# Moving the modulation sums of a four-layer block from VectorE to GpSimd

## The reference

```python
cond = jax.nn.silu(c)
for i in range(DEPTH):
    mod = (cond @ w_mod[i] + b_mod[i])[:, None, :]
    shift, scale, gate = jnp.split(mod, 3, axis=-1)
    h = rms_norm(x, norm_pre_g[i]) * (1.0 + scale) + shift
    o = mixer(h, ...)
    x = x + gate * rms_norm(o, norm_post_g[i])
```

```python
top_s, top_i = lax.top_k(s, PEER_TOPK)            # s: (T, heads, 2, 128)
cand_s = top_s[:, :, 0, :, None] + top_s[:, :, 1, None, :]
cand_i = top_i[:, :, 0, :, None] * 128 + top_i[:, :, 1, None, :]
best_s, pos = lax.top_k(cand_s, PEER_TOPK)        # over 256 candidates
idx = take_along_axis(cand_i, pos)
a = gelu(einsum('cd,ced->ce', x, expert_down[idx]))
out = einsum('ce,ced->cd', softmax(best_s) * a, expert_up[idx])
```

## Time and profile before

| | |
|---|---|
| median of 3 runs | 1738.4 us (1738.04 to 1740.64) |
| the profiled execution | 1739.41 us, its span 1737.6 us |
| TensorE busy | 1393.7 us, 80% |
| VectorE busy | 1047.5 us, 60% |
| ScalarE busy | 433.1 us, 25% |
| GpSimd busy | 490.7 us, 28% |
| DMA | 591.53 MB, mean 340 GB/s |

### The profile page before, as it was taken

How to read it: one execution, slowest core, us unless ns; L and a number is a source line. 1 busy time by engine, 2 the same in 40 slices (tenths; PEclk the granted TensorE clock), 3 DMA queues, 4 the chain that set the end, 5 groups by cost and what they waited for, 6 DMA issues and landing times. The chain is left out here.

```text
span 1737.6 us, 13867 instructions
## 1 busy us (share of the span) xinstructions
PE 1393.7 (80%) x4158; PEld 717.6 (41%) x4158; DVE 1047.5 (60%) x2197; ACT 433.1 (25%) x974; POOL 490.7 (28%) x498
## 2 busy tenths in 40 slices
PE   6998988978999999999777777699787647666665
PEld 6454435444444455444354343455333312222222
DVE  3645554553233222313797998788866778877876
ACT  1221413423423421102133232132002221111111
POOL 2101210210000000000445546355344545444441
PEclk9998998989999999999897888798888878898898
DMA  9978884978556776887999989999999999999995
GB/s 386 377 256 303 312 340 171 347 282 295 213 207 219 277 265 242 290 293 265 402 361 357 413 339 403 412 400 413 410 414 414 348 412 422 421 422 421 422 421 248
DMA packets 108941, 591.53 MB, mean 340 GB/s; under 512 B 12450, under 2 KB 12706, under 8 KB 60612
## 3 DMA queue, kind: packets, MB, share of 16 engines
q0 software_dynamic: 67776, 312.56, 45.4%
q1 hardware_dynamic: 41092, 278.10, 42.2%
HBM read 589.55 MB, written 1.05 MB: 340 GB/s over the span
## 5 line engine op out<-in xcount | busy, mean ns | idle before, releaser
L948 PE MATMUL bank<-ring,hT 128*128 128x512 f32 x1888 | 866.6, 615 | 39.6 <-DVE room L1920 12.1
L948 PEld LDWEIGHTS bank<-ring,hT 128*128 128x128 f32 x1888 | 366.5, 198 | 482.2 <-issue 449.8
L877 POOL DMA_INDIRECT room<-in_peer_down,idx x92 | 102.5, 1114 | 525.1 <-DVE idx L1781 401.8
L1798 DVE CUSTOM_DVE_ANT_0 room<-room 128x1024 f32<-128x1024 f32 x180 | 218.6, 1221 | 50.6 <-DMA room<-in_pair,idx 38.4
L1203 PE MATMUL bank<-room 128*128 128x512 f32 x284 | 150.9, 676 | 96.5 <-ACT room L1493 94.2
L1813 DVE SCALAR_TENSOR_TENSOR x<-room,pcoef,x 128x1024 f32<-128x1024 f32 x121 | 155.7, 1287 | 28.0 <-DMA room<-in_peer_up,idx 27.5
L877 POOL DMA_INDIRECT room<-in_peer_up,idx x104 | 114.0, 1096 | 88.6 <-DVE pa L1798 42.3
L1203 PEld LDWEIGHTS bank<-room 128*128 128x128 f32 x284 | 57.5, 215 | 190.8 <-issue 97.2
L849 POOL DMA_DIRECT2D room<-in_w_mod x80 | 42.2, 528 | 326.3 <-DVE room L1567 206.5
L877 POOL DMA_INDIRECT room<-in_pair,idx x88 | 97.0, 1102 | 108.5 <-PE bank L1203 50.6
L927 PE MATMUL bank<-cst,room 128*128 128x128 f32 x424 | 64.7, 297 | 55.3 <-ACT room L1439 24.1
(11 more groups left out here) (304 smaller groups left out, 1527.4 us busy)
## 6 DMA issues: line engine op xcount, KB each, us to landing
ring<-in_wpk SPq DMA_DIRECT2D x248, 1024.0 KB, 7.0
room<-in_w_mod POOLq DMA_DIRECT2D x80, 512.0 KB, 8.2
room<-in_w_mod SPq DMA_DIRECT2D x8, 1024.0 KB, 15.8
room<-in_norm_post_g POOLq DMA_DIRECT2D x4, 512.0 KB, 5.0
rowb<-in_gate_bias SPq DMA_DIRECT2D x4, 512.0 KB, 9.0
room<-in_peer_up,idx POOLq DMA_INDIRECT x104, 12.5
room<-in_peer_down,idx POOLq DMA_INDIRECT x92, 12.4
room<-in_pair,idx POOLq DMA_INDIRECT x88, 14.3
```

What stands on the lines that cost most here:

```text
L877: return pool.indirect_dma_start(out=dst, out_offset=None, in_=A[table][0] if table != "pair" else A[table], in_offset=bass.IndirectOffset ...
L948: last = mm(bank[p][:, :], lhs, ring[:, h % 4, k * N:(k + 1) * N], start=(kk == 0), stop=(h == halves[-1] and k == 3))
L1798: v.tensor_tensor_reduce(out=row, in0=row, in1=u_(g // MINE), scale=1.0, scalar=0.0, op0=ALU.mult, op1=ALU.add, accum_out=pa[:, g // TOPK ...
```

## The change

GpSimd adds the shift pieces of layers 1 to 3 and the gate pieces of all layers itself (a multiply by cond in place, then an add), with two buffers of `mring`; VectorE adds the scale pieces of layers 1 to 3 through the other two buffers. GpSimd still issues all fetches, in a fixed order with its adds. Of the first 16 pieces TensorE sums two instead of six. "mod" steps are now the 24 scale pieces, placed by PIECES_AT, behind the block's own work. The first choice stands one block earlier, choice has fewer and larger VectorE instructions, with casts folded in. In the fox layer one filling block moves from behind output block 1 to in front of block 4. The last four picks form two groups of two, and the last eight `up` rows are added earlier. (Semaphores `wsT` and `gqk` become one, `dve_set`.)

```diff
             ([], ("mm", t, f"out{L}", 1), [("post1", t, L)]),
-            "gap twice"]
+            "gap" if L == 2 else "gap twice"]
 def sgu_chunks(t, L):
...
             b(1, [], [("unit", t, 0)]),
             b(2, [], [("forget", t)]),
             b(3, [], [("unit", t, 1), ("forget_sum", t)]),
+            "gap",
             b(4, [], [("quad_T", t, 0), ("quad_S", t, 0)]),
             b(5, [], quad(0)),
             b(6, [], quad(1)),
...
             "gap",
             b(0, name="ho", pre=[("merged_T", t)]), b(1, [("ffn_norm", t)], name="ho"),
             "gap",
-            b(0, name="query", pre=[("norm_in", t, 5)]),
-            b(1, [("score_T", t, 0)], name="query"),
-            b(2, [("score_S", t, 0), ("score_T", t, 1)], name="query"),
+            b(0, [] if t else [("score_T", t, 0)], name="query", pre=[("norm_in", t, 5)]),
+            b(1, [("score_T", t, 0)] if t else [("score_S", t, 0)], name="query"),
+            b(2, ([("score_S", t, 0)] if t else []) + [("score_T", t, 1)], name="query"),
             b(3, [("score_S", t, 1), ("score_T", t, 2)], name="query"),
...
 REST = LEAD[0]
-TICKS = PICKS + REST + LEAD[1]
-PIECES = [(L, third, k) for L in range(DEPTH) for third in range(3) for k in range(KC)]
-PE_PIECES = (5, 7, 9, 11, 13, 15)
-def summed_before(n):
+TICKS = PICKS + REST + 2
+FIRST = [(0, third, k) for third in range(2) for k in range(KC)]
+PE_PIECES = (5, 7)
+DVE_FIRST = len(FIRST) - len(PE_PIECES)
+DVE_PIECES = [(L, 1, k) for L in range(1, DEPTH) for k in range(KC)]
+POOL_PIECES = [(0, 2, k) for k in range(KC)] \
+    + [(L, third, k) for L in range(1, DEPTH) for third in (0, 2) for k in range(KC)]
+def first_before(n):
     return n - sum(i < n for i in PE_PIECES)
+def scales_of(L):
+    return DVE_FIRST + KC * L
+def shifts_of(L):
+    return KC * 2 * L
+def gates_of(L):
+    return KC * (2 * L + 1)
...
 def on_vector(u):
-    return u < 7 * TOPK or u % 4 == 3 or (u % 2 and (u < MINE or u >= PICKS - 8))
+    return u < 7 * TOPK or (u % 4 == 3 and u < PICKS - 4) or (u % 2 and u < MINE) \
+        or u >= PICKS - 2 or (u % 2 and PICKS - 8 <= u < PICKS - 4)
 def tick_of(g):
...
 def added_at(v):
+    if v >= PICKS - 8:
+        return tick_of(PICKS - 2) + (v - PICKS + 8) // 2
     return tick_of(v) + LEAD[v // MINE]
...
 EXP_AT = {sums_at(hh): hh for hh in range(T * PH) if hh != PH - 1}
-GROUPS = [(hh * TOPK, TOPK) for hh in range(PH)] + [(MINE + 4 * m, 4) for m in range(MINE // 4)]
+GROUPS = [(hh * TOPK, TOPK) for hh in range(PH)] + [(MINE + 4 * m, 4) for m in range(MINE // 4 - 1)] \
+    + [(PICKS - 4, 2), (PICKS - 2, 2)]
 GROUP_AT = {tick_of(g + n - 1) + 1: i for i, (g, n) in enumerate(GROUPS)}
 def group_of(v):
-    return v // TOPK if v < MINE else PH + (v - MINE) // 4
+    return next(i for i, (g, n) in enumerate(GROUPS) if g <= v < g + n)
...
         self.at += 1
-def pieces_at(mm):
-    if mm is None:
-        return 0
-    if mm[2] == "in0":
-        return (4, 4, 3, 2, 2, 2)[mm[3]]
-    return 4 + mm[3] if mm[2] == "out0" else 3
+PIECES_AT = {"in0": (0, 1, 2, 1, 1, 1), "out0": (2, 0), "in1": (1, 2, 2, 2, 1, 0), "in2": (1, 1, 1, 1, 1, 1, 1, 1)}
 def make_order():
...
                 order.append(("sines", 0))
+            for _ in range(PIECES_AT[name][n] if name in PIECES_AT else 0):
+                order.append(("mod", piece))
+                piece += 1
             order += pending
             pending = []
-            if name == "query" and n == 2:
+            if name == "query" and n == 1:
                 order.append(("choose", 0))
-                rows.tick()
-            if name == "query" and n == 3:
-                rows.tick()
-                rows.tick()
+            if name == "query" and n >= 2:
+                for _ in range(n - 1):
+                    rows.tick()
     order += pending
...
             nc.gpsimd.memset(alT[:, :], 1.0).then_inc(S("ones_set"), 1)
-            def fetch(n):
-                L, third, k = PIECES[n]
-                pool.wait_ge(S("summed"), summed_before(2 * KC if n < 2 * KC + 4 else n - 3))
-                w = A["w_mod"][L].rearrange("(p k) n -> p k n", k=KC)
-                pool.dma_start(mring[n % 4], w[:, k, third * D:(third + 1) * D]).then_inc(S(f"pool_in{n % 4}"), 16)
+            def piece_of(L, third, k):
+                return A["w_mod"][L].rearrange("(p k) n -> p k n", k=KC)[:, k, third * D:(third + 1) * D]
+            def fetch(i):
+                if i >= len(POOL_PIECES):
+                    return
+                if i >= 2:
+                    pool.wait_ge(S("pool_summed"), i - 1)
+                pool.dma_start(mring[i % 2], piece_of(*POOL_PIECES[i])).then_inc(S(f"pool_in{i % 2}"), 16)
+            def fetch_scale(i):
+                pool.wait_ge(S("summed"), DVE_FIRST + max(i - 1, 0))
+                pool.dma_start(mring[2 + i % 2], piece_of(*DVE_PIECES[i])).then_inc(S(f"pool_in{2 + i % 2}"), 16)
+            def add_piece(i):
+                L, third, k = POOL_PIECES[i]
+                pool.wait_ge(S(f"sums_init{L % 2}"), sums_set(L))
+                pool.wait_ge(S(f"pool_in{i % 2}"), (i // 2 + 1) * 16)
+                link(nc.gpsimd.tensor_tensor(mring[i % 2], mring[i % 2], const("cond", k, 1).to_broadcast([P, D]), ALU.mult))
+                if i:
+                    pool.wait_ge(S("pool_summed"), i)
+                nc.gpsimd.tensor_tensor(sums[L % 2][third], sums[L % 2][third], mring[i % 2], ALU.add) \
+                    .then_inc(S("pool_summed"), 1)
+                fetch(i + 2)
             def start_sums(L):
                 if L >= 2:
...
             start_sums(0)
             start_sums(1)
             fetch_post(0)
-            for n in range(2 * KC, len(PIECES)):
-                fetch(n)
-                if n % (3 * KC) == 3 * KC // 2 and n > 3 * KC:
-                    fetch_post(n // (3 * KC))
-                if n in (6 * KC - 1, 9 * KC - 1):
-                    start_sums((n + 1) // (3 * KC))
+            pool.wait_ge(S("summed"), DVE_FIRST)
+            for i in range(2):
+                fetch(i)
+            for i in range(2):
+                fetch_scale(i)
+            for k in range(KC):
+                add_piece(k)
+                if k % 2:
+                    fetch_scale(2 + k // 2)
+            for L in range(1, DEPTH):
+                if L > 1:
+                    start_sums(L)
+                    fetch_post(L - 1)
+                    for k in range(2):
+                        fetch_scale((L - 1) * KC + k)
+                for k in range(KC):
+                    add_piece(shifts_of(L) - KC + k)
+                    if k + 2 < KC and (L > 1 or k >= 4):
+                        fetch_scale((L - 1) * KC + k + 2)
+                for k in range(KC):
+                    add_piece(gates_of(L) - KC + k)
+            fetch_post(DEPTH - 1)
             def gather(dst, table, g):
...
             pe.wait_ge(S("cond"), 1)
-            for piece in PE_PIECES[:2]:
+            for piece in PE_PIECES:
                 piece_columns(piece, use("mod_cols", 0)[1])
             for step in ORDER:
                 kind, t = step[0], step[1]
...
                     n, p = use(*step)
                     if n >= 2:
                         pe.wait_ge(S(f"ev{p}"), n // 2)
-                    if L == 0:
-                        for piece in PE_PIECES[2:]:
-                            piece_columns(piece, p)
                     pe.wait_ge(S(f"sums_init{L % 2}"), sums_set(L))
                     for j in range(2 * KC):
-                        if j % KC == 0:
-                            pe.wait_ge(S("summed"), summed_before(L * 3 * KC + j + KC))
+                        if j == 0 and L:
+                            pe.wait_ge(S("pool_summed"), shifts_of(L))
+                        elif j == 0:
+                            pe.wait_ge(S("summed"), first_before(KC))
+                        elif j == KC:
+                            pe.wait_ge(S("summed"), scales_of(L))
                         last = mm(bank[p][:, j:j + 1], sums[L % 2][j // KC][:, (j % KC) * P:(j % KC + 1) * P],
                                   ones[:, 0:1], start=L > 0, stop=True, skip_group_check=L == 0)
                     last.then_inc(S(f"pd{p}"), 1)
...
                     n, p = use(*step)
                     if n >= 2:
                         pe.wait_ge(S(f"ev{p}"), n // 2)
-                    pe.wait_ge(S("summed"), summed_before((L + 1) * 3 * KC))
+                    pe.wait_ge(S("pool_summed"), gates_of(L))
                     mm(bank[p][:, :], ones[:, :], sums[L % 2][2][:, i * N:(i + 1) * N], start=True, stop=True) \
...
                     .then_inc(S(f"a_T{t}"), 1)
-            def add_piece(n):
-                L, third, k = PIECES[n]
+            def add_first(n):
+                _, third, k = FIRST[n]
                 if n in PE_PIECES:
                     return
                 if n == 0:
                     dve.wait_ge(S("shift_init"), 16)
```

(47 more changed lines are left out.)

38 lines of the change are left out of this document (16 added, 22 removed).

## The result

The changed kernel takes 1784.85 us (median of 4 runs, 1779.61 to 1785.97) against 1739.52 for the kernel before, ratio 1.0251 with a 95% interval of 1.0224 to 1.0278: 45 us slower. The forecast was 1747 with a range of 1724 to 1772. The profiled execution took 1785.97 us, with a span of 1784.1.

A forecast was written before the change was run, and what follows sets the result against it. TensorE and its waits bound 46 to 514 us, DMA gathers 790 to 1400. Terms 25 - 7 - 3.5 - 4.5 - 1.4 = +8.6 on the profiled 1739.4 gave 1748.0, so 1747 as median; range 1724 to 1772.

The forecast's parts named there:

- to level 1 of tile 1 at the SGU layer: From kernel start to the SGU layer's level 1: start, gates, shifts and late scale 8 together net +25 us.
- start: First projection: TensorE sums two pieces instead of six, so it begins 9 us earlier, counted as 8.5 us gained.
- gates: Layer 0's gate matmul: GpSimd finishes the gates at 103, TensorE asks at 89.5 and stands 13 us.
- shifts: Layer 1: GpSimd's shifts are done in time, and the 5.00 us wait behind them goes, counted as 4 us gained.
- scale 8: SGU layer: GpSimd fetches this weight piece late, its add ends 24.5 us late, and TensorE stands at level 1.
- What VectorE gets back: Modulated layers: 56 of VectorE's 80 later adds go, 72 us, shortening TensorE's waits by 7 us.
- filling block: Fox layer: moved in front of block 4 it covers waits there, gaining 3.5 us; missing behind the output costs nothing.
- choice: Gather phase: the earlier first choice gains 1.8 us and less VectorE work 2.7, together 4.5, bounds 0 and 13.
- end: Kernel's tail: the last four picks in groups of two finish sooner, gaining 1.4 us.
- GpSimd's price: Shift and gate pieces: each GpSimd operation takes 2.15 us, a piece 5.4 us; bounds 1.3 and 2.9 an operation.
- The two engines slow each other: Rival for the modulation phase: GpSimd's operations stretch to 2.9 us beside VectorE, +36, 1774 us; chance 0.14.

The follow-up runs named there:

- run 2: Changed kernel with GpSimd's multiply and add replaced by memsets of full length (2048 and 2560 columns), fetches and waits kept: 1757.12 us, one run.
- run 5: Layer 2's sums set and scales 8 and 9 fetched earlier: against run 2's memset kernel 1743.96 us (one run); against the changed kernel, real sums, 1775.63 us.
- run 1: Changed kernel with GpSimd's multiply and add replaced by shorter memsets of the same places, fetches and waits kept: 1748.04 us, ratio 1.0033 to the kernel before.
- run 3: Changed kernel with GpSimd's multiply as a tensor_scalar in place of a tensor_tensor with broadcast operand: 1790.56 us, ratio 1.0278 to the kernel before.
- run 8: Kernel before with two pieces on TensorE in place of six, alone: 1742.25 us, ratio 0.9991.
- run 7: Kernel before with everything of the change but the shifts and gates on GpSimd: 1734.87 us, ratio 0.9953.
- run 6: Changed kernel with real sums in some layers, full-length memsets elsewhere: layer 3 1762.77 us; layers 2 and 3 1785.39; layer 0's gates and layer 1 1758.3.

## Why the prediction was wrong, point by point

Profile against profile the loss is 46.5 us. By the prediction's own steps, in the changed kernel's trace:

| step | forecast | measured |
|---|---|---|
| to level 1 of tile 1 at the SGU layer (start, gates, shifts, scale 8) | +25 | +27.9 (185.67 to 213.56) |
| "What VectorE gets back" | -7 | +22.2 (287.54 to 337.63, less the 27.9) |
| filling block and all else up to the query projection | -3.5 | +1.5 (823.27 to 874.84) |
| choice, up to VectorE's last dot (1722.75 to 1770.90) | -4.5 | -3.4 |
| end | -1.4 | -1.7 |
| sum | +8.6 | +46.5 |

- **GpSimd's price held.** 2.15 us an operation forecast, 1.93 and 2.4 to 2.6 measured, in the mean 2.2. Its schedule too: gates of layer 0 done at 99.6 (103 forecast), the fetch of scale 8 issued at 195.75 (199.5) and landed at 205.90 (204.7). For the add the trace agrees with what the forecast cites of the Trainium skill, GPSIMD Engine Reference, section 3.1: 2.25 us was the estimate, 2.35 is what an add takes that nothing holds.
- **The hole of scale 8 was right in its place and instant**, and is shown by runs 2 and 5. In the changed kernel it is hardly seen: VectorE waits 7.72 us for the piece, and TensorE 7.11, because the held products had already made both late. That the step's +27.9 is near the forecast's +25 is in part luck: it is another sum that ends at the same place.

```profile
206.03 1.28 DVE L1621 SCALAR_TENSOR_TENSOR room<-room,cst 128x1024 f32<-128x1024 f32 x1 [7.72 <-DMA room<-in_w_mod]
...
213.56 3.73 PE L1013 MATMUL bank<-room 128*128 128x128 f32 x16 [7.11 <-DVE room L1646]
```

  The add begins at 206.03 here and at 206.65 with memsets, though the fetch was issued at 195.75 here and at 200.18 there: here it took 10.2 us to land. So the instant is that of GpSimd's queue and of the landing behind it, and in two kernels that do the same up to there it is 206.65 and 209.54.
- **The gates of layer 0**: no wait for GpSimd, where 13 us were forecast. They were done 3.4 us earlier than that, and TensorE came 18.4 us later than forecast (107.90 for 89.5), held up by the levels. With memsets it waited 8.97.
- **The step that failed is "What VectorE gets back", -7 us.** It credits VectorE with 72 us of adds and leaves the price of everything that stays on it untouched. The four level products alone took 76.7 us for 23.3 from 62 to 490 us. Against run 2, TensorE is 23.5 us later at the columns of layer 1, but only 3.5 at level 1 (213.56 against 210.11): the late scale 8 hides the loss up to it. From level 1 to the columns of layer 2 it loses 20.9 us (124.1 for 103.2), 15 of them idle and 6 by the lower clock. Another 4 us go between the add of scale 8 and level 1 (7.5 us for 3.5). With 3.4 behind the columns of layer 2 the difference to run 2 is 27.7 in all, but the 3.4 aren't seen in the run with real sums in layers 2 and 3, which takes 551.7 us from there to the wait behind choice 1 for run 2's 552.1. Memsets in layers 2 and 3 alone take the loss away, and real sums in these layers alone bring it back; real sums in layer 3 alone don't. Nor did the relief show without the holding: the wait of 5.72 us at 232.68 that was to shrink is 9.45 in run 2 and 11.18 in the changed kernel (260.03 and 265.48), and run 2 takes 103.2 us from level 1 to the columns of layer 2, where the kernel before took 101.9. Only the wait of 4.37 us is gone, in both.
- **The rival had the cause and the wrong victim.** "The two engines slow each other" stretched GpSimd's operations to 2.9 us and came to 1774 at a chance of 0.14. GpSimd's were stretched little (means of 2.38 to 2.56 for the add by tile, single ones of 3.2); VectorE's short ones were, from 0.42 to 2.56, on the path. It could have been priced from the start: 56 products of 0.42 us beside an engine that I had counted busy for 241 of 420 us, so a meeting for 57% of them and a hold of half an operation, 1.1 us, each: an estimate of 35 us. It lies near the loss by luck. 26 of the 56 met an operation, each held for 2.05 us in the mean, 53 us in all, and the runs put what reached the end at 28. Of the rule, the Trainium skill says more on another page that I didn't weigh: SBUF — State Buffer, Who interferes with whom, has it that a VectorE instruction with two SBUF inputs and a GpSimd instruction that reads SBUF exclude each other for a whole instruction, and that one which only writes doesn't. The rows at 74.28 (2.56 us for 0.41) and runs 1 and 2 (0.42 beside memsets) agree; the tensor_scalar of run 3, beside which a product took 1.25 us for 0.41 and the next ones their own 0.41 inside its 3.11 us, doesn't fit it.
- **Start, -8.5**: forecast by the engines alone. Alone it is worth 1.6 us (interval: 4.7 less to 1.6 more). TensorE then stands in front of the loads: it waits 3.31 us for the positions, and DMA is at 0.98 from 0 to 46 us in the kernel before and in run 8 alike. That the loads are the whole reason isn't shown.
- **Filling block, -3.5**: the sign was wrong. The block ahead of block 4 puts its own evacuation by ScalarE in front of the gate matmul, 5.46 us. And the block taken from behind the output had covered the normalisation there, for which I had counted nothing: its wait went from 0.44 to 5.15 us.
- **Choice, -4.5**: the wait of 11.80 fell to 4.36, as named; alone the choice is worth 6.5 to 15 us. So the size was too small. Which of its two parts gives more wasn't told apart: TensorE stands 7.9 us earlier behind choice 1 (841.03 for 848.96), and the dip of DMA at 890 to 930 us is at 0.86, hardly filled. In the changed kernel 3.4 us of the gain are seen; why less was not settled.
- **End, -1.4**: from VectorE's last dot to the end of the span 13.2 us, 14.85 before.

The runs split the loss into three: everything else -8.2 us, lateness +22 (run 2 against run 7), held VectorE +28 (the changed kernel against run 2), together +42. They are differences along one chain of runs, so that they add up proves nothing; the 3 to 4 us that are left are those by which the kernel before was slower in the series of run 7. What supports the shares is that each of the two causes was also changed by itself, the fetch order in run 5 and the holding in runs 2 and 6. Run 2 is a single execution, so its two shares are known to a few us.

## What to carry to other kernels

Before work goes from VectorE to GpSimd, list VectorE's instructions with two SBUF inputs on the path in that stretch, and price each one that meets a GpSimd operation as held until it ends. A short instruction is held as long as a long one (here 0.41 us became 2.56), and relief of VectorE's total is no measure of it. When two causes of lateness end at the same instant, removing one shows nothing there: without the holding in layers 2 and 3, the holding in layers 0 and 1 cost 1 us, since scale 8 was late in any case. Only runs with each cause alone, with both and with neither say what each costs. And a filling block moved ahead of one wait uncovers the wait behind its old place; look for what covers that one.

## What the runs showed that I had not expected

- The holding isn't by tile size: the Newton step of 128x1 (two SBUF inputs) took 632 ns in the mean for 219: six of eight took their own time, one 1.35 us and one 2.39.
- GpSimd's tensor_scalar over the same 128x1024 took 2.90 us, its tensor_tensor with a broadcast operand 1.93: the form with less to read is slower.
- A GpSimd tensor_tensor of 128x256 took 0.65 to 0.82 us in the mean, where a quarter of the long one is 0.48 to 0.64.
- Two GpSimd memsets back to back, 1.9 us of writing, left VectorE's products at 0.42.
